# Expert token rows: from one transfer per expert on the SyncE queue to pieces of eight rows issued by GpSimd, each in two column cuts

## The reference, cut to what matters

```
def _moe_swiglu(h, w_router, w_gate, w_up, w_down):
    logits = (h @ w_router).astype(jnp.float32)
    top_v, top_i = lax.top_k(logits, TOP_K)          # 2 of 8 experts per token
    top_w = jax.nn.softmax(top_v, axis=-1)
    gates = jnp.sum(jax.nn.one_hot(top_i, N_EXP, dtype=jnp.float32) * top_w[..., None], axis=-2).astype(h.dtype)
    out = jnp.zeros_like(h)
    for e in range(N_EXP):
        out = out + gates[..., e:e + 1] * _swiglu(h, w_gate[e], w_up[e], w_down[e])
    return out
```

## Time and profile before

| | |
|---|---|
| median of 3 runs | 1403.9 us |
| the profiled execution's own time | 1404.78 us |
| its span, first to last instruction | 1403.0 us |
| mean granted TensorE clock | 0.993 of full |
| PE busy | 1334.0 us, 95% of the span |
| POOL busy | 106.0 us, 8% |
| moved by DMA | 500.15 MB, mean 356 GB/s |
| of it on SyncE's queue (q1) | 471.75 MB |

### The profile page before, as it was taken

The page is one execution under the profiler, slowest core; times in us unless marked ns, Lnnn a source line. Parts: engine busy times, 40 slices in busy tenths (PEclk is TensorE's granted clock), DMA queues, the critical chain, the costliest instruction groups (busy, mean ns, idle before and its releaser), DMA issues.

```text
span 1403.0 us, 27789 instructions
## 1 busy us (share of the span) xinstructions
PE 1334.0 (95%) x12536; PEld 709.6 (51%) x12536; DVE 364.4 (26%) x459; ACT 281.4 (20%) x362; POOL 106.0 (8%) x182
## 2 busy tenths in 40 slices
PE   5999989999999999999999999999899999998885
PEld 2997766678888885333334433333233333332331
DVE  2857343655444544101000101000101101101104
ACT  2574534344334333000000000000000000000001
POOL 6200241223000001000000000000000000010010
PEclk9999999999999999999999999999999999999999
DMA  9854868899855478999999999999999999999994
GB/s 383 296 173 156 347 241 307 340 401 409 299 179 181 178 268 317 361 415 425 424 424 428 397 423 430 394 424 429 404 424 428 402 424 427 398 424 428 423 429 200
DMA packets 103254, 500.15 MB, mean 356 GB/s; under 512 B 10417, under 2 KB 14206, under 8 KB 74470
## 3 DMA queue, kind: packets, MB, share of 16 engines
q1 hardware_dynamic: 87232, 471.75, 83.8%
q10 hardware_dynamic: 13510, 18.29, 3.6%
q0 software_dynamic: 2400, 8.42, 1.5%
HBM read 478.74 MB, written 19.69 MB: 355 GB/s over the span
## 4 chain that ended last, share of the span: by engine, by line
PE 80%; DMA 15%; DVE 2%; ACT 1%; issue 1%; SPq 1%; ACTq 0%; DVEq 0%
PE ps L2423 30%; PE ps L2452 12%; PE ps L439 6%; PE ps L441 6%; PE ps L440 6%; DMA ring_a<-in_moe_up 4%; PE ps L2447 3%; DMA ring_b<-in_moe_down 3%; PE ps L1852 2%; DMA ring_a<-in_moe_down 2%; PE ps L1838 2%; DMA raw<-in_moe_down 2%; DMA ring_b<-in_moe_up 2%; PE ps L1984 1%; PE ps L1985 1%; PE ps L1986 1%
## 5 line engine op out<-in xcount | busy, mean ns | idle before, releaser
L2423 PE MATMUL ps<-ring_a,hTf 128*32 128x512 f32 (+1 forms) x2160 | 208.6, 541 | 9.7 <-DMA ring_a<-in_moe_up 5.9
L2423 PE MATMUL ps<-raw,hTf 128*32 128x512 f32 (+1 forms) x2064 | 197.3, 538 | 1.8 <-DMA raw<-in_moe_up 1.8
L1786 DVE TENSOR_TENSOR hm<-gate_bc,ps 128x384 f32<-128x384 f32 (+1 forms) x30 | 17.8, 595 | 649.5 <-PE ps L2423 648.8
L380 DVE TENSOR_TENSOR w_lo<-raw,w_hi 128x2048 fp32r<-128x2048 f32 x60 | 144.3, 2409 | 122.5 <-ACT w_hi L376 122.4
L2423 PEld LDWEIGHTS ps<-ring_a,hTf 128*32 128x32 f32 x2160 | 70.4, 110 | 144.5 <-issue 127.6
L2423 PE MATMUL ps<-ring_b,hTf 128*32 128x384 f32 (+1 forms) x1408 | 138.4, 539 | 4.1 <-DMA ring_b<-in_moe_up 2.0
L376 ACT ACTIVATE w_hi<-raw 128x2048 fp32r<-128x2048 f32 x59 | 112.6, 1913 | 121.8 <-PE ps L441 103.1
L2423 PEld LDWEIGHTS ps<-raw,hTf 128*32 128x32 f32 x2064 | 70.7, 110 | 123.4 <-issue 118.5
L439 PE MATMUL ps<-w_hi,hTh 128*128 128x512 f32 x248 | 98.6, 397 | 1.5 <-DVE w_lo L380 1.5
L441 PE MATMUL ps<-w_lo,hTh 128*128 128x512 f32 x248 | 97.1, 391 | 0.0
L440 PE MATMUL ps<-w_hi,hTl 128*128 128x512 f32 x248 | 97.0, 391 | 0.0
(11 more groups left out here) (419 smaller groups left out, 1530.2 us busy)
## 6 DMA issues: line engine op xcount, KB each, us to landing
raw<-in_w_mod SPq DMA_DIRECT2D x48, 1024.0 KB, 9.5
raw<-in_moe_down SPq DMA_DIRECT2D x22, 2048.0 KB, 29.4
ring_a<-in_moe_down SPq DMA_DIRECT2D x20, 2048.0 KB, 21.7
ring_a<-in_moe_up SPq DMA_DIRECT2D x14, 2048.0 KB, 27.2
ring_b<-in_moe_down SPq DMA_DIRECT2D x14, 2048.0 KB, 28.0
raw<-in_moe_gate SPq DMA_DIRECT2D x13, 2048.0 KB, 25.8
ring_a<-in_moe_gate SPq DMA_DIRECT2D x11, 2048.0 KB, 32.6
raw<-in_moe_up SPq DMA_DIRECT2D x10, 2048.0 KB, 18.7
```

The costliest lines, as they stand in the source:

```text
L380: nc.vector.tensor_tensor(w_lo[:, w % SPLIT], raw[:, slot % RAW], w_hi[:, w % SPLIT].bitcast(F32), ALU.subtract).then_inc(s["lo_ready"], 1)
L1786: VT(hm[:, g, 0:w], sgm[at % SILUS][:, 0:w], ps[:, part % 4, 0:w], ALU.mult).then_inc(s["h_ready"], 1)
L2423: last = MM(ps[TOK * j:TOK * j + TOK, part % 4, 0:w], hTf1[:, kt, q * P + TOK * g:q * P + TOK * g + TOK], wt[:, kt % 2, j, :], start=kt == ...
```

## The change

The row loads leave SyncE's queue. GpSimd reads the seven expert numbers and issues the loads in a loop over the passes, position by position, after its wait for `rows_sent`. A position's rows are cut into pieces of eight, and every piece into two transfers, columns 0 to 1020 (eight pieces of 4080 bytes) and the last four columns (eight pieces of 16 bytes). 608 rows make 76 pieces and 152 transfers, where there were 7. Each transfer adds 16 to `xrow_loaded`, and TensorE waits for the sum that belongs to its position. The wait for the turn before stands once per position, ahead of its pieces.

```diff
+ROWS = 8
+ROW_CUTS = (slice(0, D - 4), slice(D - 4, D))
+LOADS = (0, *(len(ROW_CUTS) * TOK * g // ROWS for g in POS_G[1:]))
+LOAD_SUM = tuple(sum(LOADS[:i + 1]) for i in range(N_EXP))
...
-            def row_load(p, i, e):
-
-                if p == 0 and i == 1:
-                    sp.wait_ge(s["rows_sent"], 64)
-                sp.wait_ge(s["xg_turned"], N_EXP * p + i)
-                n = TOK * POS_G[i]
-                src = rows_io.rearrange("(e r) n -> e r n", r=REGION)[e, p * n:p * n + n]
-                sp.dma_start(xrow[0:n, :], src).then_inc(s["xrow_loaded"], 16)
...
                         experts.append(nc.sync.value_load(order[0:1, r:r + 1], min_val=0, max_val=N_EXP - 1))
-                        row_load(p, i + 1, experts[i + 1])
...
+            def load_rows(p, i, e):
+
+                pool.wait_ge(s["xg_turned"], N_EXP * p + i)
+                n = TOK * POS_G[i]
+                rows_e = rows_io.rearrange("(e r) n -> e r n", r=REGION)
+                for r in range(0, n, ROWS):
+                    for cut in ROW_CUTS:
+                        pool.dma_start(xrow[r:r + ROWS, cut], rows_e[e, bass.ds(n * p + r, ROWS), cut])\
+                            .then_inc(s["xrow_loaded"], 16)
+
             pool.wait_ge(s["route_ready"], 2)
+            experts = [0]
+            for r in POS_RANK[1:]:
+                experts.append(nc.gpsimd.value_load(order[0:1, r:r + 1], min_val=0, max_val=N_EXP - 1))
             passes = nc.gpsimd.value_load(npass[0:1, 0:1], min_val=1, max_val=3)
+            pool.wait_ge(s["rows_sent"], 64)
+            with pool.Fori(0, passes) as p:
+                for i in range(1, N_EXP):
+                    load_rows(p, i, experts[i])
...
-                pe.wait_ge(s["xrow_loaded"], 16 * ((N_EXP - 1) * p + i))
+                pe.wait_ge(s["xrow_loaded"], 16 * (LOAD_SUM[N_EXP - 1] * p + LOAD_SUM[i]))
```

## The result

| | before | changed |
|---|---|---|
| median of 4 runs each | 1403.84 us | 1417.36 us |
| range of the runs | 1401.48 to 1406.29 | 1413.48 to 1418.68 |
| profiled execution: its own time | 1404.78 us | 1417.72 us |
| its span | 1403.0 us | 1416.1 us |

The ratio is 1.0086, with a 95% interval of 1.0073 to 1.0100: the change makes the kernel 0.9% slower, 12 us by the ratio, where 14 were forecast (1418). Of all executions behind this text one, of the experiment e7, took 1983.7 us at a granted clock of 0.655; no ratio counts it.

A forecast was written before the change was run, and what follows sets the result against it. The prediction took the DMA engines' work on the weight stream as the bound. Its terms, -9.6 + 21.9 + 1.6 = +13.9 us on 1404.78, gave 1418.7, forecast as 1418 (0.9 lower for the median); own range 1408 to 1428, overall 1399 to 1446.

The forecast's parts named there:

- The bound: Whole kernel: the DMA engines' work on the weight stream decides the end; TensorE's waits leave room for a 10 us gain.
- Row loads leave SyncE's queue: SyncE's weight queue: seven issues go, one holding the queue for 7.74 us; worth nothing in itself.
- The dips go: Expert stage: five rate dips at the loads of positions 3 to 7 vanish, -9.6 us at most, 0 at least.
- the ports: Offered reason for the dips: 128 partitions hang on 16 ports, the first 64 reach only eight; estimated loss 0.6 us.
- 76 pieces: Expert stage: 608 rows in eight-row pieces at the dearest narrow-load price, 36 ns a row, cost 21.9 us.
- Rival B: Expert stage: crowding, eight-row writes cost 72 ns a row, +36 us, 1440, or 1446 with uneven engines; chance 0.18.
- rival A: Expert stage: pieces spread thin disturb nothing, -8 us, 1396, or 1402 with uneven engines; chance 0.18.
- Small packets and completions: DMA engines: 608 packets of 16 bytes and 145 more transfers, about 9 ns a packet, cost 1.6 us.
- Uneven engines: End of the stream: large transfers may always meet the same eight DMA engines, 5.9 us more; 0 if halves alternate.
- GpSimd's time: GpSimd's issues: 18 to 35 us for a position's 32 transfers, covered by at least 89.5 us between turns.
- Rival C: GpSimd late: 32 transfers one after another take 112 us, TensorE waits 23 us, up to 1430; chance 0.06.
- The prediction's own alternative with the uneven engines: Whole kernel: the forecast with the uneven engines' 5.9 us added, 1424; half of the forecast's 0.50.

The follow-up runs named there:

- e7: Kernel before, with SyncE issuing the rows in pieces of eight, one transfer of all columns each (76 transfers): 1411.12 us, ratio 1.0037.
- e5: Changed kernel with pieces of 16 rows in place of eight, same two column cuts (76 transfers): 1408.72 us, ratio 1.0027 to the kernel before.
- e6: Changed kernel with one GpSimd transfer per position, always of 128 rows (seven transfers): 1395.05 us, ratio 0.9925 to the kernel before.
- e12: Changed kernel with one GpSimd transfer per position of exactly the 64, 96 or 128 rows needed: 1400.06 us, ratio 0.9962 to the kernel before.
- e4: Kernel before, with every SyncE row load reading and writing 128 rows whatever the position needs: 1396.85 us, ratio 0.9949.
- e8: Kernel before, plus 152 GpSimd transfers of eight 16-byte pieces each, row loads staying on SyncE: 1405.28 us, ratio 1.0001.
- e1: Changed kernel with each eight-row piece in one transfer of all 1024 columns (76 transfers): 1414.78 us, ratio 1.0080 to the kernel before.
- e3: Changed kernel with the small transfer first in every piece: 1415.17 us, ratio 1.0077 to the kernel before.

## Why the prediction was right

*The bound.* Right. The stream of weights sets the end: in the kernels of the table the last landing moved and the work behind it hardly did (1.7 us in e5's trace, by the clock), and a gain of 11 us was taken in full by TensorE (e6), as the room in its waits had promised.

*Row loads leave SyncE's queue: nothing.* Not shown, and incomplete. The 7.74 us issue of the earlier trace rows is gone, and the sum closes without a gain from it. But e12, which differs from the kernel before in the queue alone, gains 5.3 us by the ratio. That is what its smaller dips give (4.3 us for 9.55), an effect of the queue that the prediction didn't have.

*The dips go: -9.6 us.* Right, and for the reason given, width: e4 removes them by width alone and gains what was worked out, 1397 expected and 1396.85 measured. The reason that the prediction offered for it, the ports, no run tested.

*76 pieces: +21.9 us at 36 ns a row.* Right in size: 19.2 us by the stretches, over the tens of us in which GpSimd issues, position 2's too, as was forecast. The price was 35 ns, but the 36 ns were charged for 608 rows, and position 1's 64 come before 604 us, where the stream isn't full yet (a share of 0.92 in 547 to 604 before the change). The reason for choosing the dearest row, that the price rises as the load gets narrower, doesn't hold below 64 rows: from GpSimd it is the same with eight rows as with four, and from SyncE eight rows cost 20 ns, less than its 64-row loads (29 and 36). So that the dearest row of SyncE's loads met the price of GpSimd's pieces is luck. Rival B, 72 ns a row, fails on the 35 ns measured, and rival A, which needed less than 13, too.

*Small packets and completions: +1.6 us.* Nothing, by e8 (0.9991 to 1.0011, so at most 1.5 us).

*Uneven engines: 0 or 5.9 us, left out of the sum.* This is the term that was sized wrongly by being left out: the end lost 11.2 us instead of 6.0, 5.2 more. Its reason was wrong too. At the end the rate was that of two engines, with one cut and with two, alternating or not, from GpSimd and from SyncE alike (45 to 53 GB/s in e1 to e3 and e7). By the rule of the Trainium skill ("DMA: Bandwidth & Descriptors", section "Why a DMA increments its semaphore by 16 and not by 1") the large transfers would keep to one half of the engines, and half of all engines would be late; the traces don't agree. They don't name engines, so which ones are late, and why four-row pieces leave some four behind and 16-row pieces some seven, wasn't found.

*GpSimd's time: covered.* Right. TensorE waited for no row in the changed kernel. GpSimd's issues, around position 2 and 3 (start, length, what, and idle time before), show that the cover was used, though:

```profile
615.91 0.52 POOL L816 DMA_DIRECT2D xrow<-rows_io  x1 [0.47 <-issue]
624.20 0.52 POOL L816 DMA_DIRECT2D xrow<-rows_io  x1 [7.78 <-issue]
624.88 9.74 POOL L816 DMA_DIRECT2D xrow<-rows_io  x16 [0.16 <-issue]
697.16 8.13 POOL L816 DMA_DIRECT2D xrow<-rows_io  x14 [62.55 <-PE ps L1849]
718.66 1.12 POOL L816 DMA_DIRECT2D xrow<-rows_io  x2 [13.37 <-issue]
```

Position 2's pieces took from 606.65 to 634.6, 28 us, between turns that are some 90 us apart. Rival C was far off.

That the forecast came within 1 us is luck as well. In the sum three errors nearly cancelled: 2.7 us too many for the pieces, 1.6 for the small packets, and 5.2 too few for the end. The prediction's own alternative with the uneven engines, 1424, had this last term nearly right and would have been 7 us too high.

## What to carry to other kernels

Where weights stream at the full rate of the DMA engines, a side transfer of whole rows can cost more than its bytes when it writes fewer than 128 partitions. In this kernel pieces of four and eight rows from GpSimd cost some 30 ns for each 4 KB row on top of the 10 ns of its bytes, the same rows from SyncE about 20, and a padded transfer over all 128 partitions only its bytes, from either queue. So look for short dips in the stream's rate at the landings of narrow loads, and try to widen them to 128 partitions, useless rows included, before moving them to another queue. Read the end of the stream as well: how many engines' worth of rate is left in the last microseconds says whether the work was spread evenly.

## What the runs showed that was not expected

- The same 64- and 96-row loads cost less from GpSimd's queue (4.3 us) than from the weights' own (9.55 us). With pieces of eight rows it is the other way round, 33 ns a row from GpSimd and 20 from SyncE. No run tells why.
- A piece's row count shows in the number of engines that are late at the end: four rows leave 99 to 107 GB/s, eight rows 45 to 53, 16 rows and more, and whole loads, 158 to 215. It isn't monotone, and it stays open.
- GpSimd stalls in the middle of its issues, with no wait in the program: 7.78 and 13.37 us in the rows above, and later 6.42 (from 928.6) and 11.96 (from 1034.6), each time after 31 transfers (16 + 15, 17 + 14, and so on), and in e5 too, with 16 rows (11.12 and 11.32 us after 31 each). Here it was hidden; a kernel that issues many small transfers from GpSimd against a deadline would have to count them.
